# Sums over the partitions by two single-pass matmuls of a split operand, in a fused hybrid block on one Trainium2 core

## The reference, cut to what matters

```python
# HGRN2: mean of squares over the 128 channels of a head
y_hg = rmsnorm(o_hg, hg_norm_g[l]) * silu(hg_g)
# mLSTM: the normaliser sums the weights s over the source positions ...
den = jnp.sum(s, axis=-1) + jnp.einsum('bthd,bhd->bht', qc, n) * inter_w
h = num / maximum(abs(den), exp(-m_t))
# ... and the mean of squares goes over the 256 channels of a head
y_ml = rmsnorm(h_ml, ml_norm_g[l]) * sigmoid(ml_o)
# SSD: mean of squares over the 256 channels of a group
y_mb = rmsnorm(y_ssd * silu(mb_z), mb_norm_g)
# rmsnorm(x) = x * rsqrt(mean(x * x) + 1e-6) * gain
```

## Time and profile before

| | us |
|---|---|
| median of 3 runs | 1667.75 (1667.38 to 1668.54) |
| the profiled execution, its own time | 1668.24 |
| its span | 1666.4 |

### The profile page before, as it was taken

How to read it: one execution, slowest core, us unless ns; L and a number is a source line. 1 busy time by engine, 2 the same in 40 slices (tenths; PEclk the granted TensorE clock), 3 DMA queues, 4 the chain that set the end, 5 groups by cost and what they waited for, 6 DMA issues and landing times.

```text
span 1666.4 us, 21787 instructions
## 1 busy us (share of the span) xinstructions
PE 1626.3 (98%) x7802; PEld 1303.4 (78%) x7802; DVE 855.5 (51%) x1329; ACT 723.4 (43%) x1143; POOL 607.8 (36%) x254
## 2 busy tenths in 40 slices
PE   7999999999999999999999999999999999999889
PEld 6888888777877778777777878888888877777667
DVE  4788878532454551167643335444443335565651
ACT  4656665332344432354554344444343333435441
POOL 5333223343333334332233434444444443242222
PEclk9999999999999999999999999999999999999999
DMA  5222112122222223222222322323233352222112
GB/s 185 65 64 64 63 63 64 54 88 89 87 76 76 66 75 101 76 76 64 64 76 82 95 89 93 96 89 99 88 101 102 101 178 88 64 76 68 59 51 89
DMA packets 41785, 139.31 MB, mean 84 GB/s; under 512 B 4200, under 2 KB 8552, under 8 KB 41712
## 3 DMA queue, kind: packets, MB, share of 16 engines
q1 hardware_dynamic: 40080, 132.66, 25.3%
q10 hardware_dynamic: 1632, 5.64, 0.9%
HBM read 136.15 MB, written 2.13 MB: 83 GB/s over the span
## 4 chain that ended last, share of the span: by engine, by line
PE 87%; DVE 6%; ACT 3%; issue 3%; DMA 0%; DVEq 0%; ACTq 0%; SPq 0%
PE bank L397 25%; PE bank L398 25%; PE bank L399 25%; PE bank L491 2%; PE bank L618 1%; PE bank L782 1%; PE bank L762 1%; DVE s_p L1744 1%; PE bank L771 1%; DVE unit L1508 1%; DVE hgd L1525 1%; DVE s_e L1734 0%; PE bank L588 0%; PE bank L508 0%; PE bank L539 0%
## 5 line engine op out<-in xcount | busy, mean ns | idle before, releaser
L362 POOL TENSOR_TENSOR wl<-raw,wh 128x1024 fp32r<-128x1024 f32 x245 | 599.6, 2449 | 1028.0 <-ACT wh L855 1027.7
L397 PE MATMUL bank<-hh,wh 128*128 128x512 f32 x968 | 390.2, 403 | 1.4 <-DVE hl L1977 1.0
L398 PE MATMUL bank<-hl,wh 128*128 128x512 f32 x968 | 382.9, 396 | 0.0
L399 PE MATMUL bank<-hh,wl 128*128 128x512 f32 x968 | 382.8, 395 | 0.0
L397 PE MATMUL bank<-yh,wh 128*128 128x512 f32 x800 | 320.9, 401 | 0.7 <-DVE yl L1779 0.5
L398 PE MATMUL bank<-yl,wh 128*128 128x512 f32 x800 | 317.0, 396 | 0.0
L399 PE MATMUL bank<-yh,wl 128*128 128x512 f32 x800 | 316.9, 396 | 0.0
L855 ACT ACTIVATE wh<-raw 128x1024 fp32r<-128x1024 f32 x241 | 253.2, 1054 | 110.8 <-DMA raw<-slabs 110.8
L397 PEld LDWEIGHTS bank<-hh,wh 128*128 128x128 f32 x968 | 182.1, 188 | 47.0 <-issue 4.1
L399 PEld LDWEIGHTS bank<-hh,wl 128*128 128x128 f32 x968 | 182.0, 188 | 44.3
L398 PEld LDWEIGHTS bank<-hl,wh 128*128 128x128 f32 x968 | 182.3, 188 | 42.0 <-issue 0.7
(11 more groups left out here) (304 smaller groups left out, 1874.7 us busy)
## 6 DMA issues: line engine op xcount, KB each, us to landing
raw<-slabs SPq DMA_DIRECT2D x245, 512.0 KB, 3.5
wb<-bias_scratch ACTq DMA_DIRECT2D x1, 3584.0 KB, 12.4
xs<-x SPq DMA_DIRECT2D x4, 512.0 KB, 6.1
out<-htn SPq DMA_DIRECT2D x8, 256.0 KB, 2.3
con<-consts ACTq DMA_DIRECT2D x1, 992.5 KB, 4.7
oneh<-onehot ACTq DMA_DIRECT2D x1, 512.0 KB, 5.6
con<-consts ACTq DMA_DIRECT2D x1, 192.0 KB, 4.6
par<-params ACTq DMA_DIRECT2D x1, 191.5 KB, 6.1
```

The source lines that it names most:

```text
L362: pool.tensor_tensor(slab(wl, i), slab(raw, i), slab(wh, i).bitcast(F32), ALU.subtract).then_inc(S["slab_split"], 1)
L397: mm(bank[:, :], wh[:, s, b, :], xh, start=first and i == 0, stop=False)
L398: mm(bank[:, :], wh[:, s, b, :], xl, start=False, stop=False)
L399: ins = mm(bank[:, :], wl[:, s, b, :], xh, start=False, stop=last and i == len(order) - 1)
```

## The change

Each of the 20 sums `ones x operand` becomes two matmuls of fp32r operands into the same bank: ones times the operand rounded to fp32r, and ones times the rounded operand's remainder. The ones are copied once into an fp32r tile `onr`, by VectorE at the start. For each sum ScalarE makes the rounded half by a copy, and VectorE the remainder by a subtraction; TensorE's waits count up to both. The numbers of the semaphores `hg_sq`, `ml_ps`, `ml_sq`, `ml_sa`, `mb_sq` and `mb_sa` follow. In mLSTM and SSD the halves lie on tiles that are free by then (`m_pl` on `m_ps`, `m_sr` on `m_sq`, `s_sr` on `s_sq`); in HGRN2 and for `m_ph` they are tiles of their own. One unused semaphore name goes. The core of the diff:

```diff
+            def sum_all(bank, h, l, sem):
+                mm(bank[:, :], onr[:, :], h, start=True, stop=False)
+                mm(bank[:, :], onr[:, :], l, start=False, stop=True).then_inc(sem, 1)
             def hg_sum(u):
-                pe.wait_ge(S["hg_sq"], u + 1)
+                pe.wait_ge(S["hg_sq"], u * 2 + 2)
+                pe.wait_ge(S["hg_sl"], u + 1)
                 wait(pe, S["hg_rs"], u * 2)
-                mm(b7[:, :], ones, sqh[:, :], start=True, stop=True).then_inc(S["hg_ss"], 1)
+                sum_all(b7, sqhi[:, :], sql[:, :], S["hg_ss"])
...
-                    pe.wait_ge(S["ml_ps"], 4 * u + 4)
-                    mm(b5[:, :], ones, m_ps[:, :], start=True, stop=True).then_inc(S["ml_num"], 1)
+                    pe.wait_ge(S["ml_ps"], 6 * u + 6)
+                    sum_all(b5, m_ph[:, :], m_pl[:, :], S["ml_num"])
...
             def ml_finish(u):
-                pe.wait_ge(S["ml_sa"], u + 1)
-                mm(b3[:, :], ones, m_sq[:, 0, :], start=True, stop=True).then_inc(S["ml_ss"], 1)
+                pe.wait_ge(S["ml_sq"], 3 * u + 3)
+                pe.wait_ge(S["ml_sa"], 2 * u + 2)
+                sum_all(b3, m_sr[:, 1, :], m_sr[:, 0, :], S["ml_ss"])
...
             def mb_finish(g):
-                pe.wait_ge(S["mb_sa"], g + 1)
-                mm(b5[:, :], ones, s_sq[:, 0, :], start=True, stop=True).then_inc(S["mb_ss"], 1)
+                pe.wait_ge(S["mb_sq"], 3 * g + 3)
+                pe.wait_ge(S["mb_sa"], 2 * g + 2)
+                sum_all(b5, s_sr[:, 1, :], s_sr[:, 0, :], S["mb_ss"])
...
 # ScalarE: hg_square, ahead of L995 in part 0
                 A(sqh[:, :], b6[:, :], ACT.Square).then_inc(S["hg_sq"], 1)
+                act.wait_ge(S["hg_sq"], u * 2 + 1)
+                A(sqhi[:, :], sqh[:, :], ACT.Copy).then_inc(S["hg_sq"], 1)
 # ScalarE: ml_part 2, ahead of the exponential L1062
+                    act.wait_ge(S["ml_ps"], 6 * u + 4)
+                    wait(act, S["ml_num"], 3 * u)
+                    A(m_ph[:, :], m_ps[:, :], ACT.Copy).then_inc(S["ml_ps"], 1)
 # ScalarE: ml_part 3, behind the two squares
+                    act.wait_ge(S["ml_sa"], 2 * u + 1)
+                    A(m_sr[:, 1, :], m_sq[:, 0, :], ACT.Copy).then_inc(S["ml_sq"], 1)
 # ScalarE: SSD, behind copy-out and slab rounding of tile 5, ahead of the silus
+                act.wait_ge(S["mb_sa"], 2 * g + 1)
+                A(s_sr[:, 1, :], s_sq[:, 0, :], ACT.Copy).then_inc(S["mb_sq"], 1)
...
 # VectorE: at the start, between L1367 and L1370
+            dve.wait_ge(S["ident_in"], 16)
+            dve.tensor_copy(onr[:, :], ones).then_inc(S["onr_set"], 1)
 # VectorE: HGRN2 part 0, between the difference of level 2 and the clamp;
 # for head 7 also ahead of its hg_y
+            def hg_rest(u):
+                dve.wait_ge(S["hg_sq"], u * 2 + 2)
+                TT(sql[:, :], sqh[:, :], sqhi[:, :].bitcast(F32), ALU.subtract).then_inc(S["hg_sl"], 1)
 # VectorE: ml_part 2, ahead of L1696
+                    dve.wait_ge(S["ml_ps"], 6 * u + 5)
+                    TT(m_pl[:, :], m_ps[:, :], m_ph[:, :].bitcast(F32), ALU.subtract).then_inc(S["ml_ps"], 1)
 # VectorE: ml_add, behind the add
+                dve.wait_ge(S["ml_sq"], 3 * u + 3)
+                TT(m_sr[:, 0, :], m_sq[:, 0, :], m_sr[:, 1, :].bitcast(F32), ALU.subtract).then_inc(S["ml_sa"], 1)
 # VectorE: mb_norm, behind the add
+                dve.wait_ge(S["mb_sq"], 3 * g + 3)
+                TT(s_sr[:, 0, :], s_sq[:, 0, :], s_sr[:, 1, :].bitcast(F32), ALU.subtract).then_inc(S["mb_sa"], 1)
```

More of the change, by code:

```diff
@@ L185, in build @@
         b2, b3, b4, b5, b6, b7 = psum[2:]
-        names = """params_in ident_in masks_in x_in0 x_in1 x_in2 x_in3 onehot_in pre_hi slab_hi slab_split slab_used acc_free0 acc_free1 zero_set
+        names = """params_in ident_in onr_set masks_in x_in0 x_in1 x_in2 x_in3 onehot_in pre_hi slab_hi slab_split slab_used acc_free0 acc_free1 zero_set
             pro_raw pro_x pro_xa pro_sq pro_rs pro_n pro_tr nrm_rs nrm_h nrm_hi nrm_lo lt_sq lt_add lt_ss lt_step x2_done lb_step
@@ L191, in build @@
             hg_silu hg_e hg_l hg_lf hg_b hg_f hg_k hg_d hg_ex hg_eb hg_x hg_tr hg_v hg_kt hg_lv hg_z hg_at hg_stp
-            hg_s hg_o hg_sq hg_ss hg_rs hg_y hg_hi hg_lo
+            hg_s hg_o hg_sq hg_sl hg_ss hg_rs hg_y hg_hi hg_lo
             ml_silu ml_tanh ml_nm ml_tr ml_v ml_dx ml_ex ml_qk ml_pt ml_num ml_nm2 ml_ps ml_em ml_h ml_dn ml_sq ml_sa ml_ss
@@ L197, in build @@
             cv_z cv_c cv_y cv_hi cv_lo
-            at_silu at_sq at_ss at_tr at_rs at_v at_n at_nh at_nl at_s at_l at_mx at_ex at_sum at_p at_pt at_pe at_o at_y
+            at_silu at_sq at_ss at_tr at_rs at_v at_n at_nh at_nl at_s at_l at_mx at_ex at_sum at_p at_pt at_o at_y
             at_hi at_lo out_tr out_ev out_dma0 out_dma1""".split()
@@ L236, in build @@
         x_ss = pr("x_ss", [P, NB, 2])
+        sb_end = scratch + 18 * 4 * T + 64
         nr_at = h_at + NF * 4 * T
@@ L245, in build @@
         wrow = ro("wrow", [AT_HEADS, W_LINE])
+        onr = arena(-(-sb_end // 64) * 64)[0]("onr", [P, P], F32R)
         hg = stage()
@@ L255, in build @@
         st_ = hm("hgst", [P, 3 * P])
+        sql = arena(area)[0]("hg_sql", [P, T], F32R)
+        sqhi = hm("hg_sqh", [P, T], F32R)
         ml = stage()
@@ L264, in build @@
         m_sq = ml("m_sq", [P, 2, T])
+        m_ph = ml("m_ph", [P, T], F32R)
+        m_pl = arena(scratch + 8 * 1280)[0]("m_pl", [P, T], F32R)
+        m_sr = arena(scratch + 8 * 1280 + 4 * 9 * T)[0]("m_sr", [P, 2, T], F32R)
         mb = stage()
@@ L270, in build @@
         s_sq = mb("s_sq", [P, 2, T])
+        s_sr = arena(scratch + 12 * 1280 + 4 * 4 * T)[0]("s_sr", [P, 2, T], F32R)
         s_rs = mb("s_rs", [P, T])
@@ L453, in _ @@
             pe.wait_ge(S["masks_in"], 16)
+            pe.wait_ge(S["onr_set"], 1)
             pe.wait_ge(S["onehot_in"], 16)
@@ L1586, in hg_part @@
                     hg_diff(2, u)
+                    if before:
+                        hg_rest(u - 1)
                     if more:
@@ L1639, in _ @@
                         conv4(J_ML0, unit[0][:, 0, :], "mlcw", "mlcb", 0)
+            hg_rest(HG_HEADS - 1)
             hg_y(HG_HEADS - 1, unit[(HG_HEADS - 1) % 2])
@@ L1686, in ml_part @@
                     TT(m_ps[:, P:T], m_p[:, P:T], m_p[:, 512:896], ALU.add).then_inc(S["ml_ps"], 1)
-                    dve.wait_ge(S["ml_ps"], 4 * u + 2)
+                    dve.wait_ge(S["ml_ps"], 6 * u + 2)
                     TT(m_ps[:, 2 * P:T], m_ps[:, 2 * P:T], m_p[:, 1024:1280], ALU.add).then_inc(S["ml_ps"], 1)
-                    dve.wait_ge(S["ml_ps"], 4 * u + 3)
+                    dve.wait_ge(S["ml_ps"], 6 * u + 3)
                     TT(m_ps[:, 3 * P:T], m_ps[:, 3 * P:T], m_p[:, 896:1024], ALU.add).then_inc(S["ml_ps"], 1)
                 elif part == 2:
+                    dve.wait_ge(S["ml_ps"], 6 * u + 5)
+                    TT(m_pl[:, :], m_ps[:, :], m_ph[:, :].bitcast(F32), ALU.subtract).then_inc(S["ml_ps"], 1)
                     dve.wait_ge(S["ml_num"], 3 * u + 3)
@@ L1708, in ml_add @@
             def ml_add(u):
-                dve.wait_ge(S["ml_sq"], 2 * u + 2)
+                dve.wait_ge(S["ml_sq"], 3 * u + 2)
                 TT(m_sq[:, 0, :], m_sq[:, 0, :], m_sq[:, 1, :], ALU.add).then_inc(S["ml_sa"], 1)
+                dve.wait_ge(S["ml_sq"], 3 * u + 3)
+                TT(m_sr[:, 0, :], m_sq[:, 0, :], m_sr[:, 1, :].bitcast(F32), ALU.subtract).then_inc(S["ml_sa"], 1)
             def ml_end(u):
@@ L1767, in mb_norm @@
             def mb_norm(g):
-                dve.wait_ge(S["mb_sq"], 2 * g + 2)
+                dve.wait_ge(S["mb_sq"], 3 * g + 2)
                 TT(s_sq[:, 0, :], s_sq[:, 0, :], s_sq[:, 1, :], ALU.add).then_inc(S["mb_sa"], 1)
+                dve.wait_ge(S["mb_sq"], 3 * g + 3)
+                TT(s_sr[:, 0, :], s_sq[:, 0, :], s_sr[:, 1, :].bitcast(F32), ALU.subtract).then_inc(S["mb_sa"], 1)
                 dve.wait_ge(S["mb_rs"], 2 * g + 2)
```

## The result

The changed kernel takes 1709.04 us (median of 4 runs, 1707.11 to 1711.47), the kernel before beside it 1667.57: a ratio of 1.0251 (1.0238 to 1.0264). It is 41.5 us slower, where +22.8 was forecast, and lies outside the forecast's range. The profiled execution took 1708.46 us, span 1706.7; TensorE's mean granted clock in it is 0.98, before 0.994.

What follows compares the result with a forecast made beforehand. The prediction took TensorE, with 87% of the path ending last, to bound the kernel. HGRN2 +12.7, mLSTM -3.1, SSD +12.2 and start +1.0 summed to +22.8 us, a median of 1690.5 us, range 1674 to 1697.

Steps and rivals of the forecast that it cites:

- What bounds the kernel: TensorE holds 87% of the path ending last; time put in front of a TensorE wait counts in full.
- What a sum saves: Two fp32r matmuls take 0.47 us instead of 0.86: 0.39 us saved for each of 20 sums, 7.8 us in all.
- mLSTM: Copies and subtractions there are covered by other work, so its 8 sums save 0.39 us each: -3.1 us.
- The price of the subtraction: VectorE's subtraction takes 0.69 us clear of GpSimd; started inside GpSimd's op, it ends 0.56 us after that op.
- Rival 1: Subtractions not blocked, 0.69 us each, starting just ahead of GpSimd's op: +6.6 us, 1674.3 us; chance 0.19.
- HGRN2, heads 1 to 6: The blocked subtraction delays VectorE and so level 5's operands: 1.67 us per head, +10.0 us, the 0.39 saved being lost.
- Head 7: In HGRN2's head 7 the subtraction delays a convolution that frees the next projection's accumulator: +3.1 us.
- SSD: TensorE stands at each sum for copy and blocked subtraction: +7.7 us at three boundaries, +4.5 in the last group, +12.2.
- Start: The copy of the ones may let a second GpSimd op in, delaying VectorE's hl tiles: 0 to 2.6 us, taken as +1.0.
- 12.7 - 3.1 + 12.2 + 1.0 = +22.8: Terms for HGRN2, mLSTM, SSD and start added to the profiled execution's 1668.24 us: 1691.0, median 1690.5; chance 0.62.
- Rival 3: Shifted VectorE ops meet further GpSimd ops: some 6 us on top, 1697 us and up; chance 0.08.

Runs made afterwards that it cites:

- e9: Kernel before with split sums in HGRN2 alone, ScalarE's copy behind L995 and the subtraction one piece earlier, ahead of level 1's scaling: 1667.76 us, ratio 1.0002.
- e7: Kernel before with split sums in HGRN2 alone, the subtraction replaced by a maximum with one operand read from PSUM (wrong remainder): 1674.46 us, ratio 1.0043.
- e6: Kernel before with split sums in HGRN2 alone, plus 6 unused matmuls ahead of level 5 in each head: 1681.78 us, ratio 1.0088.
- e5: Kernel before with split sums in SSD alone, plus 16 unused matmuls ahead of the waits of each SSD sum: 1679.57 us, ratio 1.0072.
- e2: Kernel before with split sums in mLSTM alone, the old fp32 sums in HGRN2 and SSD: 1665.16 us, ratio 0.9982.
- e13: The whole changed kernel plus unused matmuls, 16 before each SSD sum and 6 before each level 5: 1689.84 us, ratio 1.0133 to the kernel before.
- e10: Kernel before with split sums in SSD alone, the subtraction replaced by a maximum with one operand read from PSUM (wrong remainder): 1679.89 us, ratio 1.0072.
- e12: Kernel before with e9's HGRN2, the change's mLSTM, old SSD, and the copy of the ones behind VectorE's other start operations: 1664.31 us, ratio 0.9982.

## Why the prediction was wrong

By its own steps:

- **What bounds the kernel.** Right: the stalls arose where they were named. The rule laid down there, that a microsecond ahead of a TensorE wait counts in full, is where it went wrong: here it counted nearly double.
- **What a sum saves.** Right where it can be seen: mLSTM came 3.2 us shorter in the trace, 2.9 alone (forecast 3.1). In heads 1 to 6 of HGRN2 nearly all of the 0.39 is lost even without stalls (e9), which the prediction said only for its own placement.
- **The price of the subtraction.** Right: 2.88 us in HGRN2, 0.54 us behind GpSimd, and 0.69 in mLSTM. Rival 1 (not blocked) fell with the same rows; e7 comes near to what it would have been for HGRN2, +6.8 us (forecast in that rival 4.4), of which some 2.8 are again the clock: 1.5 behind level 5 of head 4, and 1.3 in head 7 (320 to 330 us: 0.66). The Trainium skill (SBUF — State Buffer, "SBUF: two separate sides") gave the rule by which the op with a PSUM operand escapes, and e7 agrees (0.69 us inside GpSimd's op).
- **HGRN2, heads 1 to 6.** From level 6 of one head to level 5 of the next it is 29.53 us instead of 27.75 (112.62 to 142.15, before 108.94 to 136.69): +1.78, forecast 1.67. From level 5 to level 6 it is 8.13 us instead of 6.60 (before 136.69 to 143.29): +1.53, in six heads 9.2 us, of which the prediction has nothing. e6 takes it away by keeping TensorE busy, with level 5 no earlier.
- **Head 7.** +4.6 instead of 3.1. The projection behind the convolution waits 2.96 us for it, and behind this wait, too, the clock halves; in the step of 0.43 us that costs the other 1.5:

```profile
320.65 0.47 PE L405 MATMUL bank<-hh,wh 128*128 128x512 f32 x1 [2.96 <-DVE unit L1536]
...
322.00 0.63 PE L406 MATMUL bank<-hl,wh 128*128 128x512 f32 x1
322.43 0.63 PE L407 MATMUL bank<-hh,wl 128*128 128x512 f32 x1
```

- **SSD.** The sum starts 4.70 us late, forecast 4.8. The boundaries cost +4.4, +4.3 and +4.8 instead of 2.6, the last group +6.6 instead of 4.5: about 2 us each at half clock. e5 regains 9.3.
- **Start.** +0.4 instead of +1.0, and even that is not the copy's price. The copy of the ones was itself blocked and took the place of the blocked L1370; no second GpSimd op got in between. e2 and e9 have the copy in the same place and are 0.5 and 0.2 us earlier than the kernel before at 27 us. From 14 to 22 us the clock is 0.79 in those two and in the kernel before, and 0.57 in the changed kernel:

```profile
15.69 1.91 DVE L1395 CAST onr<-con 128x128 fp32r<-128x128 f32 x1
17.52 0.15 DVE L1398 TENSOR_TENSOR lbt<-par 128x8 f32<-128x8 f32 x1
```

The step that failed is the sum itself: "12.7 - 3.1 + 12.2 + 1.0 = +22.8" has no term for TensorE's clock. Its four terms came to 22.0 us once the clock was held up (e13), and the clock made it 41.5. The price of TensorE's stalls was thus sized rightly; what they do to the clock was not priced at all. Rival 3, the only one that went as high, named another mechanism (further blocked operations), which the traces don't show. The trace of before held the warning: in head 7 of HGRN2 it has one longer wait, of 2.5 us at level 5, and behind it this window, at a clock of 0.60:

```profile
316.00:320.00 4.00, 4.00 (x16) 3.33 (x16) 3.52 (x8) 2.23 (x5) 2.46 (x1) 0.60 0.00 0
```

The prediction lengthened the waits of six heads and made four new ones in SSD without reading what stood behind this one: 8.11 us from level 5 (315.81) to level 6 (323.92), against 6.60 in head 2. Those 1.5 us in seven heads are 10.6, and the transposes L634 and L639 (1.04 and 1.06 us at full clock), twice as long at three boundaries of SSD, add 6.3: 1707. That is an estimate made with the result in hand.

Open is how the loss before level 5 divides between the 0.68 us behind ScalarE's copy and the block: no run moves the copy alone. Open, too, is why waits of equal length have half clock behind them in one place and not in another (e7, e10).

## What to carry to other kernels

A new stall of TensorE in a stretch where it was busy costs its length, and may cost as much again behind it: look in the trace of before for the longest stall there, and read the granted clock and the matmuls' steps after it. Before an operation is put beside the bottleneck, its place in both queues counts more than its length: the same copy and subtraction cost 24.7 us in one place and nothing in another. And where the bottleneck arrives earlier at an operand that is late anyway, what was saved is waited away.

## What the runs showed of the hardware

- In the changed kernel the granted clock fell from 1.00 to 0.50 for some 3.4 us behind a wait of 1.41 us, whose end came 2.5 us after the end of one of 0.36, though TensorE was busy throughout from there on. Behind a wait of 0.55 us at the same place before, and behind one of 1.31 us in SSD, it stayed at 1.00. In SSD a wait of 4.70 us had some 4 us at half clock behind it.
- The length of the single wait doesn't decide it. Of six waits of some 0.8 us in e7 one had half clock behind it and five had not (in e9 none of six); of four of 3.0 us in e10 three had it. Head 7's 2.96 us halved the clock in the changed kernel, and 2.95 us at the same place in e6 left it at 1.00, as this window of e6 over its head 7 shows:

```profile
300.00:330.00 30.00, 26.46 (x148) 22.38 (x147) 23.44 (x37) 10.67 (x21) 8.20 (x4) 1.00 0.21 64
```

The Trainium skill (TensorE: Matmul & The Clock Gate, "What's actually happening") says that the clock follows how busy the engine has been of late; the traces agree (82 to 160 us: 0.96 with the stalls, 1.00 in e6, which fills them).

- Matmuls whose result nobody reads, put into a stall, made the kernel faster by 9.3 us (e5), 11.0 (e6) and 19.2 (e13 against the changed kernel).
- At half clock a matmul of 128x512 with its weight load goes at a step of 0.43 us, at full clock at 0.23.
- VectorE's copy of 128x128 from fp32 to fp32r is blocked by GpSimd too: it ends 0.08 us after GpSimd's op both in the changed kernel (1.91 us, until 17.60) and in e12 (2.42 us, until 28.86); an operation of the subtraction's form with one operand in PSUM is not (0.69).
